# The second chunk's attention beside the first chunk's gathers

## The reference

```python
h = layer_norm(x, ln_in_g, ln_in_b)
for l in range(2):
    qa, ka, va, qb, kb, vb = split(h @ w_in[l])          # 8 + 2 + 2 and 8 + 2 + 2 heads of 64
    qa, ka = rope(rms_norm(qa, qn_g[l])), rope(rms_norm(ka, kn_g[l]))
    oa = global_attention(qa, ka, va)                    # softmax over all 256 keys
    ob = window_sink_attention(qb, kb, vb, sink[l], slopes)
    oa = rms_norm(oa, gn_a_g[l])                         # over each head's 64 values
    ob = rms_norm(ob, gn_b_g[l])
    h = layer_norm(ALPHA * h + concat([oa, ob]) @ w_o[l], ln1_g[l], ln1_b[l])
    h = layer_norm(ALPHA * h + peer_ffn(h, ...), ln2_g[l], ln2_b[l])

def peer_ffn(xc):                                        # a chunk of 128 tokens
    q = (xc @ wq).reshape(128, 8, 2, 128)
    sc = einsum('chpd,hpnd->chpn', q, sub_keys)          # scores against 2 x 128 keys a head
    s1, i1 = top_k(sc[:, :, 0], 16); s2, i2 = top_k(sc[:, :, 1], 16)
    top_s, pos = top_k(all 256 sums of s1 and s2, 16)
    eidx = 128 * i1[pos] + i2[pos]                       # 8 heads x 16 experts for each token
    a = gelu(einsum('chkd,cd->chk', u[eidx], xc))
    return einsum('chk,chkd->cd', softmax(top_s) * a, v[eidx])
```

## Time and profile before

| | us |
|---|---|
| median of 3 runs | 2925.54 (2920.96 to 2927.78) |
| the profiled execution | 2928.04 |
| its span | 2926.2 |
| PE, DVE, POOL, ACT busy | 2148.5, 1582.8, 843.2, 813.4 |
| gathers of layer 0, layer 1 (stages) | 260 to 944, 1155 to 1833 |

### The profile page before, as it was taken

How to read it: one execution, slowest core, us unless ns; L and a number is a source line. 1 busy time by engine, 2 the same in 40 slices (tenths; PEclk the granted TensorE clock), 3 DMA queues, 4 the chain that set the end, 5 groups by cost and what they waited for, 6 DMA issues and landing times.

```text
span 2926.2 us, 33545 instructions
## 1 busy us (share of the span) xinstructions
PE 2148.5 (73%) x11740; PEld 1089.7 (37%) x11740; DVE 1582.8 (54%) x3254; ACT 813.4 (28%) x2292; POOL 843.2 (29%) x723
## 2 busy tenths in 40 slices
PE   6988677666766989676767666789878677667573
PEld 3657111121211559232323221568764532222221
DVE  4426857678544645888979865455552522121111
ACT  1402343433433212343343533322210111111110
POOL 1001444445432100454445553012110111222221
PEclk9889687677866989688888997899989788888887
DMA  7744999999999414999999999412112599999994
GB/s 282 263 169 159 421 422 422 420 412 395 422 422 378 194 37 160 381 421 375 413 378 403 422 421 417 159 42 74 58 62 101 210 404 401 388 391 381 382 379 146
DMA packets 130146, 891.48 MB, mean 305 GB/s; under 512 B 23216, under 2 KB 23600, under 8 KB 31792
## 3 DMA queue, kind: packets, MB, share of 16 engines
q0 software_dynamic: 86976, 553.74, 46.9%
q1 hardware_dynamic: 42992, 335.50, 28.6%
HBM read 880.21 MB, written 40.37 MB: 315 GB/s over the span
## 4 chain that ended last, share of the span: by engine, by line
PE 33%; DMA 33%; DVE 25%; ACT 4%; issue 4%; POOL 2%; SPq 1%; DVEq 0%; ACTq 0%; POOLq 0%
PE ps L155 31%; DMA ring<-in_peer_uv,idx_u 18%; DVE ring L1343 8%; DMA ring<-in_w_gu 6%; DVE arena L76 6%; DMA ring<-in_w_down 3%; ACT arena L125 3%; DMA arena<-in_w_gu 2%; PE ps L158 2%; DVE iu L113 2%; DVE arena L109 2%; DVE arena L1343 1%; DMA arena<-in_w_down 1%; DVE arena L97 1%; DMA arena<-in_peer_uv,idx_u 1%
## 5 line engine op out<-in xcount | busy, mean ns | idle before, releaser
L155 PE MATMUL ps<-ring,arena 64*64 64x512 f32 (+4 forms) x5248 | 1057.6, 764 | 475.2 <-ACT arena L125 348.0
L1343 DVE CUSTOM_DVE_ANT_0 ring<-ring,h 128x1024 f32<-128x1024 f32 x448 | 561.3, 1253 | 298.2 <-DMA ring<-in_peer_uv,idx_u 264.5
L2424 POOL DMA_INDIRECT ring<-in_peer_uv,idx_u x448 | 500.6, 1117 | 676.6 <-PE ps L155 517.4
L155 PEld LDWEIGHTS ps<-ring,arena 64*64 64x64 f32 (+3 forms) x5248 | 264.2, 158 | 1118.3 <-ACT arena L125 762.2
L155 PE MATMUL ps<-arena 128*128 128x128 f32 (+7 forms) x2760 | 471.4, 434 | 133.7 <-ACT arena L125 65.8
L125 ACT ACTIVATE arena<-arena 128x1 f32<-128x1 f32 (+3 forms) x1093 | 294.2, 269 | 812.8 <-DVE arena L1343 693.2
L155 PEld LDWEIGHTS ps<-arena 128*128 128x128 f32 (+4 forms) x2760 | 290.2, 191 | 325.4 <-ACT arena L125 150.7
L76 DVE TENSOR_TENSOR arena<-arena,ps 128x512 f32<-128x512 f32 (+1 forms) x158 | 93.6, 593 | 429.3 <-ACT arena L125 356.3
L155 PE MATMUL ps<-ring,hT 128*128 128x512 f32 (+2 forms) x896 | 310.2, 507 | 15.2 <-DVE hT L97 9.7
L125 ACT ACTIVATE arena<-ps 128x512 f32<-128x512 f32 (+5 forms) x192 | 106.4, 554 | 754.9 <-PE ps L155 707.5
L155 PEld LDWEIGHTS ps<-ring,hT 128*128 128x128 f32 x896 | 173.8, 200 | 140.9 <-issue 115.2
(11 more groups left out here) (116 smaller groups left out, 1394.6 us busy)
## 6 DMA issues: line engine op xcount, KB each, us to landing
ring<-in_w_gu SPq DMA_DIRECT2D x98, 1024.0 KB, 28.5
ring<-in_w_down SPq DMA_DIRECT2D x52, 1024.0 KB, 30.7
ring<-in_w_in SPq DMA_DIRECT2D x16, 2048.0 KB, 12.5
arena<-in_w_gu SPq DMA_DIRECT2D x30, 1024.0 KB, 29.9
ring<-in_w_mod SPq DMA_DIRECT2D x12, 2048.0 KB, 7.8
ring<-in_peer_wq SPq DMA_DIRECT2D x8, 2048.0 KB, 7.8
ring<-in_w_o SPq DMA_DIRECT2D x6, 2048.0 KB, 10.4
ring<-in_w_gates SPq DMA_DIRECT2D x12, 1024.0 KB, 4.9
```

Of the source, the lines that this page charges most:

```text
L155: return self.e.matmul(o, lhsT, rhs, start=start, stop=stop, skip_group_check=True)
L1343: v.done(v.e.tensor_tensor_reduce(out=row, in0=row, in1=h[:, n // 128, :], scale=1.0, scalar=0.0, op0=ALU.mult, op1=ALU.add, accum_out=aa[ ...
L2424: g.e.indirect_dma_start(out=landing(n), out_offset=None, in_=d["peer_uv"], in_offset=bass.IndirectOffsetOnAxis(ap=idx_u[:, n:n + 1], axis ...
```

## The change

The two chunks are no longer taken together. `attention(l)` becomes `first_chunk(l)`, which does for chunk 0 all that must be done before its rows can be gathered: keys and values of both chunks, attention of chunk 0, output projection, layer norm, queries, key scores. `second_chunk(l)` is a generator that does the same for chunk 1 as the first part of `background`, and `next_rows(1)` makes the projections, keys and queries of layer 1's chunk 0 as the last part of layer 0's `background` (chunk 0 is finished at n = 138). The columns of `w_in` are reordered so that keys and values are the first block. `beside` takes a step in two of three gathers below n = 72, and more of the later ones than before.

The attention itself changes form. Heads are worked in pairs, one of each key head, on the two halves of the partitions; the powers are scaled before they are turned; `values` leaves its result transposed, 64 values of a head in 64 partitions, so the mix needs no transposes. The norm over a head is then a sum over partitions: ACT squares, `spread` sums with a matmul of ones, which leaves the sum in all 64 partitions, and the root is made on that whole tile.

Each `wq` block is loaded twice (chunk 0, chunk 1), since its place is needed between. The modulation blocks move from four places each in the ring to halves in places 0 to 3, which are landing places of gathers 6 and 7. The core of the diff:

```diff
+    if n < 72:
+        return 1 if n >= 2 and n % 3 else 0
     if l:
-        return 1 if n in range(10, 250, 3) else 0
-    return 1 if n in range(10, 246, 6) else 0
+        return 1 if n < 250 and n % 2 == 0 else 0
+    return 1 if n in range(72, LAST_ROWS, 3) or n in range(LAST_ROWS, 252, 2) else 0
...
+            def spread(l, br, c, among=range(8)):
+                b = fresh("ms", l, br, c, among=among)
+                pe.wait_ge(*at("sq", "mix", l, br, c))
+                for kv in range(2):
+                    d_ = slice(64 * kv, 64 * kv + 64)
+                    t = pe.mm(b[d_, :], C("ones")[d_, 0:64], spread_at(br, c)[0][d_, :])
+                pe.done(t, ("ps", "ms", l, br, c))
...
+            def mean_squares(l, br, c):
+                v.wait_ge(*at("ps", "ms", l, br, c))
+                v.ts(spread_at(br, c)[1], tile_of("ms", l, br, c)[:, :], 1.0 / 64, 1e-6, ALU.mult, ALU.add,
+                     ("mix var", l, br, c), ("out", "ms", l, br, c))
+            def mixed(l, br, c):
+                r = spread_at(br, c)[1]
+                v.wait_ge(*at("mix rstd", l, br, c))
+                for j in range(4):
+                    k = 4 * br + j
+                    v.stt(hT[:, k, c * P:(c + 1) * P], tile_of("pv", l, br, c)[:, j * P:(j + 1) * P],
+                          smalls["gn"][:, 8 * l + k:8 * l + k + 1], r[:, j * P:(j + 1) * P], ALU.mult, ALU.mult,
+                          ("mix", l, br, c), ("out", "pv", l, br, c))
...
+            def first_chunk(l):                          # DVE
...
+                maxima(l, 1, 0)
+                maxima(l, 0, 0)
+                scaled(l, 1, 0)
+                turned_powers(l, 1, 0)
+                scaled(l, 0, 0)
+                mean_squares(l, 1, 0)
+                turned_powers(l, 0, 0)
+                mixed(l, 1, 0)
+                mean_squares(l, 0, 0)
+                mixed(l, 0, 0)
+                run(rope(l, "q", 1))
+                add_rows(l, 0)
+                run(norm_of(2 * l + 1, 0))
...
+            def mix_rsqrt(l, br, c):                     # POOL
+                r = spread_at(br, c)[1]
+                g.wait_ge(*at("mix var", l, br, c))
+                g.tt(r, r, mhalf[:, 0:1].to_broadcast([P, 512]), ALU.pow, ("mix rstd", l, br, c))
+            def second_chunk(l):                         # POOL
+                yield
+                for br in (1, 0):
+                    yield from idle(6)
+                    mix_rsqrt(l, br, 1)
+                    yield from idle(2)
+                yield from idle(6)
+                rsqrt(st["rs"][:, 1:2], ("var", 2 * l + 1, 1), "rstd", 2 * l + 1, 1)
+                yield from idle(3 + 1 + 18)
...
-                attention(l)
+                first_chunk(l)
                 if l:
-                    peer(l, context_states())
+                    peer(l, chain(second_chunk(l), context_states()))
                 else:
-                    peer(l, chain(context_rows(), conv_features(ctx_side, ctx_side.conv_blocks, 0)))
+                    peer(l, chain(second_chunk(l), context_rows(), conv_features(ctx_side, ctx_side.conv_blocks, 0),
+                                  next_rows(1)))
...
+                for i in range(2):                       # SP
+                    block(X_AT[l][i], 4, d["peer_wq"][l, i], ("loaded", "wq", l, i, 0), after=[("used", "w_in", l, 1 + i)])
+                if l == 0:
+                    modulate(2, 3, 4)
+                for i in range(2):
+                    block(X_AT[l][i], 4, d["peer_wq"][l, 2 + i], ("loaded", "wq", l, 2 + i, 0), after=[("used", "wq", l, i, 0)])
+                if l == 0:
+                    modulate(5, 6, 7, 8, 9, 10, 11)
+                for i in range(4):
+                    block(Y_AT[l][i % 2], 4, d["peer_wq"][l, i], ("loaded", "wq", l, i, 1),
+                          after=[("used", "wq", l, i - 2, 1) if i > 1 else ("used", "w_o", l, i)])
+                    if i == 1:
+                        norm_rows(4 + 4 * l, "ln2", l, [("used", "ln1", l)])
...
+                    elif i >= 6 and l == 0:              # gather(n) on POOL
+                        for half in range(2):
+                            g.wait_ge(*at("used", "w_mod", 11, half))
```

More of the change, by code:

```diff
@@ L466, in heads_mm @@
                 pe.done(t, *names)
[L468 to L484, removed]
-                        for k in range(8):
-                            t = pe.mm(b[:, :], hT[:, k, c * P:(c + 1) * P], R(4 * i, 4)[:, k * 512:(k + 1) * 512],
-                                      k == 0, k == 7)
-                        pe.done(t, ("ps", "proj", l, i, c))
-                    pe.tell(("used", "w_in", l, i))
-                free = range(7) if l == 0 else range(8)
-                upper = (4, 5, 6) if l == 0 else (4, 5, 6, 7)
@@ L555, in attention @@
+                turned_powers(l, 1, 0, free)
                 modulation(1)
-                scores(1, 1, upper)
+                values(l, 1, 0, free)
+                turned_powers(l, 0, 0, free)
+                spread(l, 1, 0, free)
                 modulation(2)
-                turned_powers(1, 0, upper)
+                values(l, 0, 0, free)
+                spread(l, 0, 0, free)
+                run(out_rows(l, 0, free))
                 modulation(3)
-                scores(0, 1, (0, 1, 2, 3))
+                turned_queries(l, 0, 1, free)
@@ new lines, in first_chunk @@
+                modulation(8, 9, 10, 11)
+                modulation_columns(2)
+            def second_chunk(l):
+                yield
+                for br in (1, 0):
+                    scores(l, br, 1, OTHERS)
+                    yield from idle(3)
+                    turned_powers(l, br, 1, OTHERS)
+                    yield from idle(2)
+                    values(l, br, 1, OTHERS)
+                    yield
+                    spread(l, br, 1, OTHERS)
+                    yield from idle(2)
+                yield from out_rows(l, 1, OTHERS)
+                yield from idle(5)
+                turned_rows(2 * l + 1, 1, OTHERS)
+                yield
+                for hf in range(2):
+                    for i in (2 * hf, 2 * hf + 1):
+                        yield from queries(l, i, 1, OTHERS)
+                        yield
+                    key_scores(l, 1, hf, OTHERS)
+                    yield
@@ new lines, in second_chunk @@
+            def second_chunk(l):
+                if l == 0:
+                    mod_columns()
+                biases(1)
+                yield
+                for br in (1, 0):
+                    maxima(l, br, 1)
+                    yield from idle(2)
+                    scaled(l, br, 1)
+                    yield from idle(2)
+                    turned_powers(l, br, 1)
+                    yield from idle(2)
+                    mean_squares(l, br, 1)
+                    yield
+                    mixed(l, br, 1)
+                    yield
+                yield from idle(4)
+                add_rows(l, 1)
+                yield from norm_of(2 * l + 1, 1)
+                v.tell(("used", "ln1", l))
+                yield from idle(2 + 18)
```

1023 lines of the change are left out of this document (556 added, 467 removed).

## The result

| | before | after |
|---|---|---|
| median of 4 runs, us | 2924.74 (2920.96 to 2927.78) | 3630.26 (3627.58 to 3635.53) |
| ratio, 95% interval | | 1.2415 [1.2394, 1.2437] |
| span of the profiled execution | 2926.2 | 3625.3 |
| PE, DVE, POOL, ACT busy | 2148.5, 1582.8, 843.2, 813.4 | 2115.9, 1593.5, 1491.9, 823.8 |

The change makes the kernel 24% slower. The forecast was 3447 us, 18% slower, with 3290 to 3620 as its own range and 3150 to 3630 as the wide one; the median lies at the upper end, just beyond both. PE, DVE and ACT are busy for about as long as before. POOL has 649 us more, and the span has 699 us more.

The account below looks back on a forecast made before the run. Gathers wait only for DMA, stages around them for a serial PE, DVE and ACT chain. 2928.0 - 71 - 67 + 42 + 30 = 2862, plus 2 x 150 + 288 for powers: 3450, by the median 3447 us; range 3290 to 3620, wide 3150 to 3630.

Parts of the forecast that it names:

- The stage between the gathers, -71, and the first stage: Chains ahead of each layer's gathers, rebuilt for one chunk: first gather 71 us earlier in layer 1, 67 in layer 0.
- The price of `pow`, P = 80 us: Each of eight 128x512 POOL powers in `mix_rsqrt` takes 0.39 + 512 x 0.156 = 80 us, extrapolated from few columns.
- Where the powers fall: Two powers in a row ahead of each gather stage, +150 us per layer; two within it, 72 us each, +288 in all.
- The wait of gather 6, +10: Layer 0: gather 6 waits for the last modulation product, whose block loads come late; 10 us with the restart.
- What it adds to the gather stages: Both gather stages: extra loads of 37 and 22 us, plus 5 and 8 for DVE, together +42 and +30 us.
- PE's share is covered: Gather stages: PE's 64x64 matmuls leave over half of each 2.49 us free at full clock, so no cost was added.
- Context work now starts behind n = 72: First 72 gathers: moving context work behind them leaves some 28 us of DVE free in layer 1.
- A: The eight powers: long `pow` runs like a multiplication, giving 2860 us, faster by 2.3%; chance 0.13.
- B: The eight powers: P is in between, 40 us at half the slope, giving 3127 us; chance 0.05.
- C: Powers in `second_chunk` are hidden because enough gathers are in flight, giving 3159 us; chance 0.04.
- E: Stages ahead of the gathers: the change doesn't shorten the chains because queue orders undo it, 3585 us; chance 0.04.
- D: First 72 gathers: DVE becomes the bound, +37 to +74 us for a layer, 3485 to 3560; 0.74 together with the forecast.

Follow-up runs that it names:

- e2: Changed kernel with the eight 128x512 roots made on ACT as exp(-0.5 ln x) instead of POOL's pow, nothing left out: 3001.61 us, ratio 1.0253.
- e1: Changed kernel with the eight 128x512 POOL pow operations replaced by multiplications of the same shape, place and queue: 3001.21 us, ratio 1.0259.
- e9: From e2, modulation blocks 5, 7 and 9 land in the arena places of gathers 0 and 1, so loads come two at a time: 2980.54 us, ratio 1.0186.
- e12: From e9 plus spaced steps and later routing: second chunk's ACT exponentials and roots replaced by lighter operations, values wrong: 2954.48 us, ratio 1.0092.
- e13: From e9 plus spaced steps and later routing: second chunk's query projections sum 2 of 8 feature parts: 2978.99 us, ratio 1.0179.
- e6: Kernel before, with only layer 1's context steps moved to every second gather from n = 72, not every third from 10: 2949.57 us, ratio 1.0086.
- e14: From e12, also leaving out much of the second chunk's output projection, turned powers, value products and DVE scaling; hand-overs kept: 2925.24 us, ratio 0.9997.
- e7: From e2, second loads of the query blocks bring 512 of 4096 columns, so chunk 1's queries are wrong: 2986.87 us, ratio 1.0218.
- e4: Changed kernel with pow kept only in second_chunk's four roots, the first chunk's four made multiplications as in e1: 3316.18 us, single run.
- e8: From e2, DVE's pieces of route(1) moved from every second gather in 2 to 48 to every gather in 30 to 53: 2992.37 us, ratio 1.0231.

## Why the prediction was wrong

Its direction and its main mechanism, the power, held. A smaller step, what the change adds to the gather stages, had the wrong mechanism, and that is most of the error. It gave 522 us over the kernel before, and the profile has 699. The 177 us between them are 122 in that step, 13 in the wait of gather 6, 38 in the powers and 4 behind the last gather. By its own steps:

- **The stage between the gathers, -71, and the first stage.** e2 has -72 and -76, against -71 and -77. These were the terms that were worked out operation by operation. Only their sums are compared here, not their parts.
- **The price of `pow`, P = 80 us.** 81.92 to 81.96 measured, eight times. A straight line through one, four and eight columns held to 512.
- **Where the powers fall.** +150 a layer ahead of the gathers and +72 each behind them; after minus e2 gives 156.5 and 158.7, and 153.7 and 156.6 for a pair. So 78 each in both places, 626 us in all instead of 588. The five gathers in flight hide less than the 11 us that I took off: for the power at 437.23 the last two of them had been issued 12 us earlier, because POOL waited 10.22 us for DVE's `mean_squares` before it could start. Such a wait stands in e1 too (7.29 us), so it isn't the power's.
- **The wait of gather 6, +10.** It was +23 (n = 6 is 39.3 us behind the first gather in e2, 16.0 before). Mis-sized, not missed; e9 gets 21 us back.
- **"What it adds to the gather stages", +42 and +30: the step that failed.** It adds +123 and +94 (e2), of which 23 are that wait: 194 instead of 72. The step priced traffic (59 us) and 13 us for DVE, because "DVE is close to the bound but mostly not over it". It asked which engine is full. None is. It left out that the attention's steps stand in series on the path of each gather, in pieces of 5 to 8 us. Lighter pieces on ACT, which it didn't price at all and which is busy under half of the time, gave back 27 us (e12), and on PE and DVE another 29 (e14). "PE's share is covered" held for the queries (e13); how much of the 29 us is PE's wasn't tried apart.
- **Also left out there: where the context work goes.** "Context work now starts behind n = 72" was taken as room gained in the first gathers. The later ones pay 32 us for it in layer 1 (e6). Layer 0 has its own form of it, with `next_rows` and a denser `beside`: its gathers 72 to 255 are 42 us longer in e2, of which its 6.29 MB of `w_in` are 15 us by traffic. The rest of that wasn't tried apart.

For layer 1 of e2 the parts are, in order of gathers: 18 us for n = 0 to 30, of which e14 gives back 17 (99.3 us in e2, 82.5 in e14), though against e6 the loss is 28 and 11 of it stay; 32 for 30 to 72, of which e14 gives back 11 (133.5 us in e2, 123.0 in e14), while the other 21 are the size of the traffic's 20 (taking seven eighths of that traffic out of e2 gave 4.7 there, e7, so the two don't simply add); 45 for 72 to 255, of which 32 are the squeezed context as e6 has it. The other 13 us have no experiment of their own. Layer 0 has none either for 27 of its 42 us, so a good part of the step's error stays open.

Of the rivals, A and B fell with the first POOL row, C with e4, E with e2's chains. D, "DVE becomes the bound of the first 72 gathers", named the right place and about the right price, and the wrong cause: with DVE's routing moved away (e8) only 9 us came back. The sign it gave, DVE above 92% over the first 72 gathers, isn't there either: DVE is busy 71 of 99 and 76 of 133 us in layer 1 of e2.

The stated range has a fault of its own. The two spreads, -121 to +152 for P and +-50 for the schedule, added to 3447 straight give 3276 to 3649; 3290 to 3620 is narrower, and the forecast doesn't say why. The +-50 fell short as well: without the powers the sum was off by 139 us (3001 in e2's profiled execution, 2862 in the forecast).

## What to carry to other kernels

A norm whose means are spread over partitions turns a root on 8 columns into one on 512; where that is wanted, look first at what the engine's power costs for each column, and give it to ACT. Work put beside a queue of transfers must be costed on every engine that a transfer's data passes, as time in series with each transfer, and not by the engines' busy shares. And moving one thing into a stage moves out another, whose new place has a price too.

## What the runs showed of the hardware

POOL's `pow` on 128x512 took 81.92 to 81.96 us, 0.16 us a column, and a multiplication of that shape 1.27, and 1.03 to 1.04 in the very places of the powers (e1). In the kernel after, one of two columns took 0.73 to 0.82 us and one of eight 2.09 to 2.16, where the earlier trace rows have 1.64 for eight; these 0.5 us stay unexplained.

DVE's dots that start together with one of the four powers among the gathers take 2.06 us each time, where the median of all dots is 1.23 (a few others are slow too, up to 2.84). After, DVE:

```profile
437.28 2.06 DVE L1466 CUSTOM_DVE_ANT_0 ring<-ring,h 128x1024 f32<-128x1024 f32 x1
...
519.22 1.51 DVE L89 SCALAR_TENSOR_TENSOR hT<-ps,small,arena 128x128 f32<-128x128 f32 x4 [78.16 <-POOL arena L134]
520.87 1.23 DVE L1466 CUSTOM_DVE_ANT_0 ring<-ring,h 128x1024 f32<-128x1024 f32 x1
```

In e1, where a multiplication of 1.04 us stands in the power's place, the dots that start with it take the same 2.06 us:

```profile
280.86 1.04 POOL L134 TENSOR_TENSOR arena<-arena,cst 128x512 f32<-128x512 f32 x1 [7.29 <-DVE arena L84]
...
280.92 2.06 DVE L1466 CUSTOM_DVE_ANT_0 ring<-ring,h 128x1024 f32<-128x1024 f32 x1
```

So these dots, which have two SBUF operands, are slowed by 0.83 us beside a POOL operation of 82 us as beside one of 1 us, and are not kept out until the power ends. By the Trainium skill (SBUF — State Buffer, Terms, "shared port pair") DVE and GpSimd hold that pair exclusively for a full instruction and the loser is blocked; the four rows beside a power don't agree with that.

ACT changed its table in 1.28 us, and the next operation began 0.02 us later (1165.08 and 1166.38 above). The Trainium skill (ScalarE: Activation LUTs, What ACT_TABLE_LOAD costs) gives about 1.28 us for the load, which agrees, and about 2.66 us for the whole switch with a drain, which these rows don't show.
